# Start addresses of the weights' and the activations' halves moved by 32 or 64 bytes

## The reference

```python
def first_block(x, ...):
    for l in range(2):
        x = x + 0.5 * swiglu(rms_norm(x, ffn1_norm[l]), ...)
        x = x + hybrid_mixer(rms_norm(x, mix_norm[l]), ...)
        x = x + 0.5 * swiglu(rms_norm(x, ffn2_norm[l]), ...)
    return rms_norm(x, final_norm)
```

## Time and profile before

| | |
|---|---|
| median of 3 runs | 2849.26 us (2848.96 to 2849.78) |
| the profiled execution | 2849.65 us |
| its span, first to last instruction | 2847.9 us |
| mean granted TensorE clock | 0.999 of full speed |
| PE / weight loads / DVE / ACT / POOL busy | 99 / 88 / 64 / 51 / 8 % |
| read from HBM | 500.12 MB, 176 GB/s |

### The profile page before, as it was taken

How to read it: one execution, slowest core, us unless ns; L and a number is a source line. 1 busy time by engine, 2 the same in 40 slices (tenths; PEclk the granted TensorE clock), 3 DMA queues, 4 the chain that set the end, 5 groups by cost and what they waited for, 6 DMA issues and landing times.

```text
span 2847.9 us, 44506 instructions
## 1 busy us (share of the span) xinstructions
PE 2822.8 (99%) x18116; PEld 2502.8 (88%) x18116; DVE 1815.2 (64%) x2700; ACT 1450.6 (51%) x2238; POOL 238.0 (8%) x187
## 2 busy tenths in 40 slices
PE   9999999999999999999999999999999999999998
PEld 8989879989989779989988887899799888878997
DVE  6646665646655676645468777665555687777655
ACT  5445555445445545444456555444344465655442
POOL 0010001010010011010013100010100131000100
PEclk9999999999999999999999999999999999999999
DMA  6544444545544445555555444555555454445553
GB/s 239 191 167 157 153 148 177 191 179 189 196 164 146 151 151 199 190 194 194 185 187 178 149 156 159 198 199 183 186 199 192 167 195 150 161 153 184 204 199 119
DMA packets 74779, 504.09 MB, mean 177 GB/s; under 512 B 8752, under 2 KB 10448, under 8 KB 18768
## 3 DMA queue, kind: packets, MB, share of 16 engines
q1 hardware_dynamic: 74576, 501.24, 49.2%
HBM read 500.12 MB, written 1.08 MB: 176 GB/s over the span
## 4 chain that ended last, share of the span: by engine, by line
PE 92%; DVE 4%; POOL 1%; ACT 1%; issue 1%; DMA 0%; SPq 0%; DVEq 0%; ACTq 0%
PE ps L1524 45%; PE ps L1542 39%; PE ps L1563 3%; POOL wlo L2452 1%; DVE conv L2281 1%; PE ps L1658 1%; DVE wlo L1987 1%; PE ps L1656 1%; PE ps L1683 1%; ACT whi L1728 0%; ACT conv L1898 0%; DVE ps L2098 0%; DVE stat L2103 0%; PE ps L1673 0%; PE ps L1674 0%
## 5 line engine op out<-in xcount | busy, mean ns | idle before, releaser
L1728 ACT ACTIVATE whi<-raw 128x1024 fp32r<-128x1024 f32 (+3 forms) x938 | 976.8, 1043 | 868.4 <-PE ps L1524 435.2
L1987 DVE TENSOR_TENSOR wlo<-raw,whi 128x1024 fp32r<-128x1024 f32 (+2 forms) x894 | 1080.6, 1220 | 301.9 <-ACT whi L1728 300.7
L1542 PE MATMUL ps<-xT_hi,whi 128*128 128x256 f32 x3296 | 927.3, 281 | 2.1 <-DVE wlo L1987 1.1
L1542 PE MATMUL ps<-xT_lo,whi 128*128 128x256 f32 x3296 | 920.5, 279 | 0.0
L1542 PE MATMUL ps<-xT_hi,wlo 128*128 128x256 f32 x3296 | 919.7, 279 | 0.0
L1542 PEld LDWEIGHTS ps<-xT_hi,whi 128*128 128x128 f32 x3296 | 619.4, 188 | 9.5 <-issue 6.9
L1542 PEld LDWEIGHTS ps<-xT_lo,whi 128*128 128x128 f32 x3296 | 619.7, 188 | 0.5
L1542 PEld LDWEIGHTS ps<-xT_hi,wlo 128*128 128x128 f32 x3296 | 619.4, 188 | 0.0
L1524 PE MATMUL ps<-whi,xT_hi 128*128 128x512 f32 (+2 forms) x1152 | 368.3, 401 | 1.5 <-DVE xT_lo L2006 0.8
L1524 PE MATMUL ps<-wlo,xT_hi 128*128 128x512 f32 (+2 forms) x1152 | 355.3, 389 | 0.2
L1524 PE MATMUL ps<-whi,xT_lo 128*128 128x512 f32 (+2 forms) x1152 | 355.1, 389 | 0.0
(11 more groups left out here) (316 smaller groups left out, 2365.5 us busy)
## 6 DMA issues: line engine op xcount, KB each, us to landing
raw<-in_w SPq DMA_DIRECT2D x436, 1024.0 KB, 4.8
vr<-in_vrows SPq DMA_DIRECT2D x19, 512.0 KB, 5.7
raw<-in_w SPq DMA_DIRECT2D x12, 768.0 KB, 4.2
raw<-in_w SPq DMA_DIRECT2D x10, 896.0 KB, 4.5
sums<-scratch SPq DMA_DIRECT2D x8, 512.0 KB, 4.5
raw<-in_w SPq DMA_DIRECT2D x4, 832.0 KB, 4.5
raw<-in_w SPq DMA_DIRECT2D x4, 576.0 KB, 3.7
x<-in_x SPq DMA_DIRECT2D x2, 512.0 KB, 6.4
```

The lines of the kernel that those rows point to most:

```text
L1542: made = e.matmul(out, ws[:, o:o + 128], xs[:, kt, :], start=kt == 0 and n == 0 and c % 2 == 0, stop=kt == job.nk - 1 and n == 2, skip_gro ...
L1728: e.activation(out, raw, ACT.Copy).then_inc(*mark("hi", i))
L1987: e.tensor_tensor(out, raw, hi.bitcast(F32), sub).then_inc(*mark("lo", i))
```

## The change

`halves` now allocates 64 bytes per partition (`_step`, never used) between the upper and the lower half of each pair of activations. The rings whi and wlo get an unused buffer of 64 bytes (whi) or 32 bytes (wlo) between one buffer and the next. No instruction is added, removed or moved; addresses behind these fillers shift. By the rule of allocation above the starts, modulo 256 bytes, become:

| buffer | before | after |
|---|---|---|
| raw0 to raw2 | 128 | 128 |
| whi0 to whi4 | 128 each | 128, 192, 0, 64, 128 |
| wlo0 to wlo4 | 128 each | 128, 160, 192, 224, 0 |
| x, xn, ident, cols | 128 | 0 |
| xT_hi, xT_lo | 160, 160 | 32, 96 |
| hT1 and hT2, hi, lo | 192, 192 | 128, 192 |
| oTa hi, lo | 192, 192 | 128, 192 |
| oTb hi, lo | 192, 192 | 192, 0 |
| oT2 hi, lo | 64, 64 | 0, 64 |

```diff
--- before.py
+++ after.py
@@ -248,16 +248,21 @@
         return m[name]
 
     def halves(name, nk, scope=ctx):
-        m[name] = Halves(name, sbuf(name + "_hi", [128, nk, 256], F32R, scope),
-                         sbuf(name + "_lo", [128, nk, 256], F32R, scope), nk)
+        hi = sbuf(name + "_hi", [128, nk, 256], F32R, scope)
+        sbuf(name + "_step", [128, 16], F32, scope)
+        m[name] = Halves(name, hi, sbuf(name + "_lo", [128, nk, 256], F32R, scope), nk)
 
     def many(name, n, shape, dt=F32, scope=ctx):
         m[name] = [sbuf(f"{name}{i}", shape, dt, scope) for i in range(n)]
 
     m["ps"] = [ctx.enter_context(nc.psum_tensor(f"ps{i}", [128, 512], F32)) for i in range(8)]
     many("raw", NRAW, [128, BLOCK])
-    many("whi", NHL, [128, PIECE], F32R)
-    many("wlo", NHL, [128, PIECE], F32R)
+    m["whi"], m["wlo"] = [], []
+    for name, step in (("whi", 16), ("wlo", 8)):
+        for i in range(NHL):
+            m[name].append(sbuf(f"{name}{i}", [128, PIECE], F32R))
+            if i < NHL - 1:
+                sbuf(f"{name}{i}_step", [128, step])
     many("x", 2, [128, D])
     sbuf("xn", [128, 2, D])
     sbuf("ident", [128, 128])
```

## The result

The changed kernel takes 2862.52 us (median of 4 runs, 2861.49 to 2863.12); the kernel before, beside it on the same chip, 2849.36 (2848.96 to 2849.78). The ratio is 1.0045, with a 95% interval of 1.0032 to 1.0057: slower by 0.45%, where 0.31% faster had been forecast.

A forecast was written before the change was run, and what follows sets the result against it. PE was taken as the bound, through the distance between matmul starts. Terms -5.8 + 1.2 - 4.3 = -8.9 us on the median 2849.26 gave 2840.4 us; own range 2831 to 2847, over cases 2806 to 2866.

The forecast's parts named there:

- What bounds the kernel: PE, busy 99%: time is matmul count times start-to-start distance; clock at its upper level from end to end.
- That addresses count: Matmul streams: distance depends on where operands begin; oT2 in L1524 takes 229.0 ns, xT 233.3.
- the neighbours of rows 6: L1524's successive xT and oT2 pieces, alike but for the stationary operand's start: distance falls by 4.3 ns.
- rival A: Whole kernel: nothing moves, 2849 us, oT2's faster distance perhaps coming from elsewhere; chance 0.22.
- Step 1, L1524: 512-column matmuls: one in four new offsets good, -5.8 us; oT2's matmuls lose theirs for three in four, +1.2 us.
- Step 2, L1542: 9888 matmuls of 256 columns: gain 0.43 ns each as L1557 shows, -4.3 us; bounds -21.5 and +11 us.
- Steps 3 and 4: Halving on ACT and DVE, POOL's L2452, and the DMAs: 0 us; at most 3 us and 1 us either way.
- Rival B: Matmul streams: alternating offsets break the rhythm, the 117.8 ns form becomes the rule; +5 to +25 us, middle 2862; chance 0.28.
- Rival C: L1524 and L1542: fixed offsets are poor, most others like oT2's; much faster, 2815 us; chance 0.13.
- D: All matmuls: most of the 214 us surplus over pure streaming goes; half of it gives 2742 us; chance 0.05.

The follow-up runs named there:

- x_at_64: Kernel before plus unused fillers ahead of xT, hT and oT2, putting all activations at 64 modulo 256, weights staying at 128: 2820.95 us, ratio 0.9900.
- x192_h0: Kernel before with fillers resized: activations' start less weights', modulo 256, is 192 for xT, 0 for hT, oTa, oTb, oT2: 2812.19 us, ratio 0.9867.
- x0_h128: Kernel before with fillers: activations' start less weights' is 0 for xT, 128 for hT, oTa, oTb, 224 for oT2: 2865.28 us, ratio 1.0054.
- shift384: Kernel before plus one unused buffer of 384 bytes behind wlo4, whi and wlo all staying at 128: 2856.21 us, ratio 1.0024.
- x160_h224: Kernel before with fillers: activations' start less weights' is 160 for xT, 224 for hT, oTa, oTb, 0 for oT2: 2864.53 us, ratio 1.0049.
- x96_h96: Kernel before with fillers: activations' start less weights' is 96 modulo 256 for all activations: 2885.13 us, ratio 1.0124.

## Why the prediction was wrong

*What bounds the kernel*: right. The time moved by the distance between matmuls, PE waits at no place for more than 5.2 us in all after (5.8 before), and its share stayed 99%. One reading was wrong, without weight for the sum: the upper level of the clock does not hold from end to end, it is left for 3.4 us at 1048.2 us, and again at the very end, when PE is done.

*That addresses count* (the neighbours of rows 6, rival A against it): right, and shown: oT2's 229.0 ns went with its offset 192. Moved to 64 or 96 oT2 stands at 233 to 234 ns, while xT and hT come down to 229 or 229.5 when they are put at 192, hT1 in x_at_64 excepted. The Trainium skill's page SBUF — State Buffer, section "Who interferes with whom", gives independent read ports and a PE that never waits; taken as a forecast that starts don't matter, it does not hold for float32r in this kernel: ratios from 0.987 to 1.012 came from unused buffers alone.

*Step 1, L1524*: right. Forecast -5.8 + 1.2 = -4.6 us, measured -5.9. One in four offsets was taken as good, a choice without a measurement; the table has two of eight (0 and 192), 0 better than the one I had seen. So the sign rests on what the rows showed, and the closeness of the size is partly luck. hT x258 was to be near 59.9 and came at 59.65, oT2 "towards 16.7" and came at 16.73.

*Step 2, L1542*: this is the step that failed. It took -0.43 ns from L1557 as "the nearest row", -4.3 us; measured +1.8 ns, +17.8 us. L1557 has 16 columns to load where L1542 has 128, and its 24 matmuls average over four offsets (32, 96, 160 and 224). At these four the table gives L1542 118.4 ns on average, where L1557 has 116.25, so at like offsets the wide loads cost 2 ns more. The row was near in its offsets and far in what meets at them. That it took 2.79 us both before and after does not mean that offsets leave it alone: in x192_h0 and x_at_64, where its offsets are 0, 64, 128 and 192, it takes 2.73 us, 113.75 ns, and in x0_h128, at the same four, 2.81. Its upper bound, the slow pieces' 117.8 ns or +11 us, was too low as well: it was the worst that one offset had shown, and other offsets go to 120. So the failure is one of sign and of bound, both because the trace had L1542 at a single offset: x-w 32, which the table now ranks second. A change that leaves a good offset for a mix loses. Nor does the mix run through all multiples of 32, as the prediction says: in L1542 the matmuls' own offsets are six of the eight, all but 0 and 192, so that the best is left out; the table weighs them to 118.3 ns.

*Steps 3 and 4* (ACT, DVE, POOL, DMA at nothing): right.

*Rival B*: its time, 2862, was the measured one, but by luck, not for its reason. It had the alternation break the rhythm and slow form 117.8 ns as the worst. L1542 went to 118.75, and shift384 has no alternation at all and is at 118.0. The rhythm itself is real: x_at_64 and x192_h0 show 113.4 and 117.8 ns at one and the same offset. *Rival C*, "most others are like oT2's", fell; *D* too: no long piece came below 113.3 and 226.7 ns on average.

## What stays open

Whether the matmul meets its own operand's load or the next one's was not separated: with constant starts the two offsets are the same. In the trace after, the offset of the load that follows sorts the distances of L1542 somewhat better (a spread that is left of 2.28 ns against 2.41, of 2.69 in all), and the means of its classes lie within 1.5 ns of the table, those by the matmul's own load within 2.5; no more than a hint. Why the first block falls into 117.8 ns at x-w 192 and the second into 113.4 is open too; before L1542's long pieces there stand four matmuls of the row scale in the first block, four transposes in the second, but no run changed that. In the first block of x_at_64 the 72 matmuls ahead of the row scale take 8.18 us, 113.6 ns, and the 864 behind it 117.8, with the same xT; so the break, or what stands in it, has a part in the choice. The 0.4 ns by which the whole change is slower in L1542 than its table may be the mixing.

## What to carry to other kernels

Where PE is the bound, in a float32r kernel like this one, the only one tried, the difference between the start of the stationary and of the moving operand, modulo 256 bytes, is a parameter to tune: here it is worth 1.3% one way and 1.2% the other, for a few unused bytes. Choose it by a sweep of constant offsets for each shape of matmul (the best x-w was 192 for L1542 and 0 for L1524), and keep the operands of a group alike; spreading them averages over good and bad. When a trace shows a resource at one setting only, neither that setting's extremes nor a smaller operation at other settings bound what the others cost.

## What was not expected of the hardware

- A stream of equal matmuls with constant offsets runs in repeating patterns of starts. Mean distances for 256 columns, over 864 or 936 in a row: 113.4, 116.7, 117.3, 117.8, 118.3, 118.7 and 120.0 ns. The same offset can hold two or three of them (x160_h224: 117.3, 118.7 and 120.0), each from one break to the next.
- At 512 columns the best constant offset was 0 (227.4 ns), at 256 columns, with the roles of the operands exchanged, 0 was next to worst (119.9).
- The writes of ACT and DVE to whi and wlo did not show in the distance: in the trace before, L1542 has 116.6 ns with ACT and DVE idle and 116.9 with both busy; in x96_h96 it has 120.0 with either, in x192_h0 115.5 and 115.4. So the differences between the offsets do not come from the work of the two engines.
- The granted clock falls to its lower level for 3.4 or 6.8 us in the middle of a kernel whose PE is 99% busy, around 420 and 1050 us, at both places in some profiles and at one in others. The 18 L1524 matmuls at 1050 us, 4.2 us at 233.3 ns each (an estimate), take 5.25 us with 3.4 us of it and 6.10 with 6.8.
